# Two attention blocks and an expert layer on one core: intermediate results kept in PSUM, one wait moved, weight units rounded earlier

## What is computed

```python
z = rms_norm(x) @ w_in                     # q, c_kv, q_idx, k_idx, w_idx, g_attn, x_rnn, g_rnn, merge
s_idx = sum_j relu(q_idx[j] @ k_idx.T) * w_idx[j]          # 8 index heads, then the 64 best keys
o     = softmax(q_lat @ c_sel.T - slope * dist) @ c_sel    # 16 heads on the normalised latent c_kv
h     = rg_lru(conv4(x_rnn))               # u = b + sum of 4 taps; gates tanh(u @ w_rg)
x     = rms_norm(x + (g_a * (o * silu(g_attn)) @ w_proj + g_r * (h * silu(g_rnn)) @ w_rproj) @ w_out)
h2    = rmsnorm(x);  x = x + mixed(moba_attention(h2), mla_attention(h2))     # 8 + 8 heads
x     = rmsnorm(x + hierarchical_moe(rmsnorm(x)))          # 32 experts, 2 per token
```

## Time and profile before

| what | us |
|---|---|
| median of 3 runs | 736.76 (736.65 to 737.17) |
| profiled execution, its time | 739.29 |
| profiled execution, its span | 737.4 |
| PE busy | 662.7 (90%) |
| DVE busy | 397.5 (54%) |
| ACT busy | 327.3 (44%) |
| POOL busy | 394.2 (53%) |
| chain that ended last | PE 46%, DVE 25%, DMA 16%, ACT 5% |
| HBM read | 179.73 MB, 245 GB/s over the span |

### The profile page before, as it was taken

How to read it: one execution, slowest core, us unless ns; L and a number is a source line. 1 busy time by engine, 2 the same in 40 slices (tenths; PEclk the granted TensorE clock), 3 DMA queues, 4 the chain that set the end, 5 groups by cost and what they waited for, 6 DMA issues and landing times.

```text
span 737.4 us, 13811 instructions
## 1 busy us (share of the span) xinstructions
PE 662.7 (90%) x5600; PEld 553.8 (75%) x5600; DVE 397.5 (54%) x672; ACT 327.3 (44%) x599; POOL 394.2 (53%) x284
## 2 busy tenths in 40 slices
PE   3999989989999999989999999999999986786763
PEld 3999879889989999988779999999655443443321
DVE  6799954699995247997955655533322111111102
ACT  7556657855653456564358755451211110011003
POOL 3889657687879989798799665881000000000000
PEclk9999999999999999999999999998999998899997
DMA  8755333433444555434364434999799999999992
GB/s 346 276 171 173 115 114 124 160 119 122 165 122 165 179 196 196 171 127 161 115 216 132 154 128 148 374 424 384 287 424 419 423 418 424 420 421 422 421 417 85
DMA packets 26130, 181.72 MB, mean 246 GB/s; under 512 B 2896, under 2 KB 3152, under 8 KB 4688
## 3 DMA queue, kind: packets, MB, share of 16 engines
q1 hardware_dynamic: 25488, 179.22, 63.6%
q10 hardware_dynamic: 576, 1.57, 0.6%
HBM read 179.73 MB, written 1.05 MB: 245 GB/s over the span
## 4 chain that ended last, share of the span: by engine, by line
PE 46%; DVE 25%; DMA 16%; ACT 5%; issue 4%; POOL 2%; SPq 2%; ACTq 0%; DVEq 0%
PE D L446 25%; DMA big<-w_expert_dram 7%; DVE big L1440 6%; PE L L881 4%; DMA ring<-w_expert_dram 4%; DMA attn<-w_expert_dram 4%; POOL ring_r L1423 2%; DVE small L1440 2%; SPq L387 2%; PE L L861 2%; PE QB L914 2%; DVE hT L1440 2%; PE L L603 2%; DVE big_r L1459 1%; DVE big_r L1464 1%
## 5 line engine op out<-in xcount | busy, mean ns | idle before, releaser
L1423 POOL TENSOR_TENSOR ring_r<-ring,ring_r 128x512 fp32r<-128x512 f32 x280 | 394.0, 1442 | 105.3 <-ACT ring_r L1030 105.2
L446 PE MATMUL D<-scr_r,ring_r 128*128 128x256 f32 x1104 | 213.1, 289 | 0.8 <-DVE big L1440 0.8
L1030 ACT ACTIVATE ring_r<-ring 128x1024 fp32r<-128x1024 f32 x140 | 146.2, 1053 | 75.7 <-PE D L446 68.5
L446 PEld LDWEIGHTS D<-scr_r,ring_r 128*128 128x128 f32 x1104 | 175.4, 191 | 3.4 <-issue 2.1
L446 PE MATMUL D<-hT_r,ring_r 128*128 128x256 f32 x552 | 156.1, 283 | 0.0
L446 PE MATMUL D<-big_r,ring_r 128*128 128x256 f32 x1110 | 138.5, 285 | 1.6 <-POOL ring_r L1423 1.6
L446 PEld LDWEIGHTS D<-big_r,ring_r 128*128 128x128 f32 x1110 | 135.0, 192 | 3.7 <-issue 2.8
L446 PEld LDWEIGHTS D<-hT_r,ring_r 128*128 128x128 f32 x552 | 105.8, 192 | 1.2 <-issue 1.0
L1440 DVE SCALAR_TENSOR_TENSOR th<-th,L 64x256 f32<-64x256 f32 x32 | 13.4, 418 | 136.6 <-ACT th L1345 136.0
L1345 ACT ACTIVATE th<-L 64x256 f32<-64x256 f32 x16 | 6.0, 377 | 91.8 <-PE L L881 91.8
L881 PE MATMUL L<-big,small 128*32 128x256 f32 x432 | 33.3, 412 | 12.3 <-DMA big<-w_expert_dram 9.3
(11 more groups left out here) (358 smaller groups left out, 1011.7 us busy)
## 6 DMA issues: line engine op xcount, KB each, us to landing
ring<-w_dense_dram SPq DMA_DIRECT2D x69, 1024.0 KB, 4.9
big<-w_expert_dram SPq DMA_DIRECT2D x40, 1024.0 KB, 26.3
ring<-w_expert_dram SPq DMA_DIRECT2D x30, 1024.0 KB, 26.5
wu<-w_expert_dram SPq DMA_DIRECT2D x6, 1024.0 KB, 25.3
scr<-w_expert_dram SPq DMA_DIRECT2D x5, 1024.0 KB, 21.8
hT<-w_expert_dram SPq DMA_DIRECT2D x5, 1024.0 KB, 23.9
attn<-w_expert_dram SPq DMA_DIRECT2D x5, 1024.0 KB, 24.1
xT<-w_expert_dram SPq DMA_DIRECT2D x5, 1024.0 KB, 26.0
```

The source lines that it names most:

```text
L446: last = mm(out_, r32(w[i][ws]), r32(x[j][xs_]), start=start and m == 0, stop=stop and m == 2)
L1030: A_(r32(hi_unit(j)), dense_unit(j), ACT.Copy).then_inc(hi_ready, 1)
L1423: last = g.tensor_tensor(r32(w), w, r32(h).bitcast(F32), ALU.subtract)
```

## The change

1. PE's first chunk takes the rest of the weight before the rest of x.
2. The relu of the index scores is written in place in PSUM; DVE reads the scores there; PE waits for the accumulation (`idx_acc`) instead of the relu before it overwrites a bank.
3. The norm of the latent moves behind the index selection on DVE, and its wait on PE moves from ahead of the q units to `values(0)`.
4. The convolution's sums stay in PSUM banks QB, UB, L0, L1 until the last tap. `rg_gates` therefore waits for all eight sums. `rg_gates` 0 and 1 come after q unit 5, the others within q units 6 and 7, after their third and sixth block and at their end. ACT takes `rg_tanh` 0 to 6, then `q_in(3)`, then 7.
5. Logits stay in banks L0 and L1 through bias, maximum and exp; `normalise` reads them there and writes E; `score_pair` waits for the previous pair's `probs` instead of its `biased`.
6. Attention outputs are gated in PSUM and split from there; `head_out` goes.
7. At the entry of the second block ACT rounds one unit ahead of the first piece of the hidden state and one each ahead of the second and third.
8. `uq` units are rounded 768 columns wide, and one of each pair before the wait for its second unit.

```diff
...
+        CB = [QB, UB, L0, L1]
...
+        def width(n):
+            return QC * P if 0 <= n - UNIT0["uq"] < H2 else UNIT
...
-            def chunk(stage, c, src, kc=DC, split=None, per=2):
+            def chunk(stage, c, src, kc=DC, split=None, per=2, between=None):
+                if between:
+                    for k in range(kc):
+                        last = mm3(dst, w, src, np.s_[:, k * P:(k + 1) * P], np.s_[:, k, :], k == 0, k == kc - 1)
+                        if k in (2, 5):
+                            between(k // 3)
+                    last.then_inc(unit_done, 1)
+                    between(2)
+                    return
...
+                pe.wait_ge(lo_ready, 1)
+                for k in range(DC):
+                    mm(dst, r32(w[1][:, k * P:(k + 1) * P]), r32(x0_hi[:, k, :]), start=False, stop=False)
-                    mm(dst, r32(w[0][:, k * P:(k + 1) * P]), r32(x0_lo[:, k, :]), start=False, stop=False)
-                pe.wait_ge(lo_ready, 1)
-                for k in range(DC):
-                    last = mm(dst, r32(w[1][:, k * P:(k + 1) * P]), r32(x0_hi[:, k, :]), start=False, stop=(k == DC - 1))
+                    last = mm(dst, r32(w[0][:, k * P:(k + 1) * P]), r32(x0_lo[:, k, :]), start=False, stop=(k == DC - 1))
...
-                        pe.wait_ge(idx_relu, j - 2)
+                        pe.wait_ge(idx_acc, j - 2)
...
-                pe.wait_ge(conv_done, c + 1)
-                pe.wait_ge(idx_relu, IDXH)
+                pe.wait_ge(conv_done, 8)
...
-                pe.wait_ge(v1_ready, n - 1) if n >= 2 else pe.wait_ge(idx_relu, IDXH)
+                pe.wait_ge(v1_ready, n - 1) if n >= 2 else pe.wait_ge(idx_acc, IDXH)
+                if n == 0:
+                    pe.wait_ge(normed, NM0[N_CKV] + 1)
-            pe.wait_ge(normed, NM0[N_CKV] + 1)
-                chunk("q", c, h2)
+                chunk("q", c, h2, between=(lambda i: rg_gates(3 * c - 16 + i)) if c >= 6 else None)
-                if c >= 6:
-                    for i in range(4 * (c - 6), 4 * (c - 6) + 4):
-                        rg_gates(i)
+                if c == 5:
+                    rg_gates(0)
+                    rg_gates(1)
-                pe.wait_ge(biased, a) if a else pe.wait_ge(gates, 8)
+                pe.wait_ge(probs, a) if a else pe.wait_ge(gates, 8)
...
+            def o_bank_emptied(n):
+                for name, size in (("o", 8), ("ob", 4), ("oa", 4)):
+                    if n <= size:
+                        break
+                    n -= size
+                pe.wait_ge(lo_of[name], n)
-                    pe.wait_ge(o_ready, a // 2 - 1)
+                    o_bank_emptied(a // 2 - 1)
...
-            pe.wait_ge(o_ready, 8)
+            pe.wait_ge(lo_of["o"], 8)
...
-                    pe.wait_ge(o_ready, 16)
+                    pe.wait_ge(lo_of["oa"], 4)
...
-                    A_(r32(hi_unit(j)), dense_unit(j), ACT.Copy).then_inc(hi_ready, 1)
+                    w = np.s_[:, 0:width(j)]
+                    A_(r32(hi_unit(j)[w]), dense_unit(j)[w], ACT.Copy).then_inc(hi_ready, 1)
...
+                if i == 2:
+                    act.wait_ge(idx_acc, IDXH)
-                    last = A_(u[:, c, :], bank[:, m * T:(m + 1) * T], ACT.Identity, bias=V("conv_b", c),
-                              scale=V("conv_w", 3 * 8 + c))
+                    last = A_(CB[i][:, m * T:(m + 1) * T], bank[:, m * T:(m + 1) * T], ACT.Identity,
+                              bias=V("conv_b", c), scale=V("conv_w", 3 * 8 + c))
-                    if j >= 4:
-                        act.wait_ge(idx_acc, j - 3)
-                    A_(scores_in[:, j % 4, :], IB[j % 4][:, 0:CAUSAL], ACT.Relu).then_inc(idx_relu, 1)
+                    A_(IB[j % 4][:, 0:CAUSAL], IB[j % 4][:, 0:CAUSAL], ACT.Relu).then_inc(idx_relu, 1)
...
-            for c in range(4):
+            for c in range(7):
-            for c in range(4, 8):
-                rg_tanh(c)
+            rg_tanh(7)
...
-                if a >= 2:
-                    act.wait_ge(pt_mm, a - 1)
-                    last = A_(E[:, a % 2, c0:c0 + n], S[:, a % 2, c0:c0 + n], ACT.Exp,
+                    last = A_(LB[a % 2][:, c0:c0 + n], LB[a % 2][:, c0:c0 + n], ACT.Exp,
...
-            round_pieces("att2", hT, scr, lambda i: act.wait_ge(normed, NM0[N_FIN1] + 2 * i + 2))
+            advance(UNIT0["cq"] + 5 + HI_UNITS)
+            def hidden_ready(i):
+                if i:
+                    advance(UNIT0["cq"] + 5 + min(i, 2) + HI_UNITS)
+                act.wait_ge(normed, NM0[N_FIN1] + 2 * i + 2)
+            round_pieces("att2", hT, scr, hidden_ready)
...
+                advance(UNITS_AT[FILL0["uq"] + i] - 1 + HI_UNITS)
...
-                    cols = np.s_[:, half * UNIT // 2:(half + 1) * UNIT // 2]
+                    cols = np.s_[:, half * width(n) // 2:(half + 1) * width(n) // 2]
...
-            dve.wait_ge(rel["dve"], 1)
-            norm(N_CKV, lambda c: zc[:, 0, :], lambda c: cT, "kv_norm_gain")
...
-                    last = stt(acc, scores_in[:, j % 4, c0:c0 + n], widx[:, tt, j:j + 1],
+                    last = stt(acc, IB[j % 4][:, c0:c0 + n], widx[:, tt, j:j + 1],
...
+            dve.wait_ge(rel["dve"], 1)
+            norm(N_CKV, lambda c: zc[:, 0, :], lambda c: cT, "kv_norm_gain")
+                taps = CB[c // 2][:, (c % 2) * T:(c % 2 + 1) * T]
-                    ins = stt(u[:, c, :], xr[:, c, 1 + t:1 + t + T], V("conv_w", t * 8 + c), u[:, c, :],
+                    ins = stt(taps if t else u[:, c, :], xr[:, c, 1 + t:1 + t + T], V("conv_w", t * 8 + c), taps,
...
-                if a >= 2:
-                    dve.wait_ge(expd, a - 1)
-                sa = S[:, a % 2, :]
+                sa = LB[a % 2][:, 0:CAUSAL]
-                    ins = stt(sa, Dm, float(2.0 ** (-8.0 * (a + 1) / H1)), LB[a % 2][:, 0:CAUSAL], ALU.mult, ALU.add)
+                    ins = stt(sa, Dm, float(2.0 ** (-8.0 * (a + 1) / H1)), sa, ALU.mult, ALU.add)
-                    ins = stt(sa, LB[a % 2][:, 0:CAUSAL], MOBA_SCALE if a < H1 + H2 else MLA_SCALE,
+                    ins = stt(sa, sa, MOBA_SCALE if a < H1 + H2 else MLA_SCALE,
-                    last = v.reduce_max(stat[:, a % 2, 0, tt:tt + 1], S[:, a % 2, c0:c0 + n], axis=AX.X, negate=True)
+                    last = v.reduce_max(stat[:, a % 2, 0, tt:tt + 1], sa[:, c0:c0 + n], axis=AX.X, negate=True)
+                if a >= 2:
+                    dve.wait_ge(pt_mm, a - 1)
-                    last = v.tensor_scalar(E[:, a % 2, c0:c0 + n], E[:, a % 2, c0:c0 + n],
+                    last = v.tensor_scalar(E[:, a % 2, c0:c0 + n], LB[a % 2][:, c0:c0 + n],
...
-                stt(oT[:, n, :], o_bank(n)[:, 0:T], 0.5, sg[:, n, :]).then_inc(o_ready, 1)
+                step(stt(o_bank(n)[:, 0:T], o_bank(n)[:, 0:T], 0.5, sg[:, n, :]))
+            def split_bank(name, lo, hi, i, bank):
+                v.tensor_copy(r32(hi[:, i, :]), bank).then_inc(hi_of[name], 1)
+                dve.wait_ge(hi_of[name], i + 1)
+                v.tensor_tensor(r32(lo[:, i, :]), bank, r32(hi[:, i, :]).bitcast(F32), ALU.subtract).then_inc(lo_of[name], 1)
-                dve.wait_ge(o_ready, n + 1)
-                split("o", oT, o_hi, n)
+                split_bank("o", oT, o_hi, n, o_bank(n)[:, 0:T])
...
-            def head_out(n):
+            def head_split(n):
-                dst = oB if n < 4 else oA
-                v.tensor_copy(dst[:, n % 4, :], o_bank(n)[:, 0:T]).then_inc(o_ready, 1)
-            def head_split(n):
-                dve.wait_ge(o_ready, 8 + n + 1)
-                split(*(("ob", oB, ob_hi) if n < 4 else ("oa", oA, oa_hi)), n % 4)
+                split_bank(*(("ob", oB, ob_hi) if n < 4 else ("oa", oA, oa_hi)), n % 4, o_bank(n)[:, 0:T])
-                if m >= 2:
-                    head_out(m - 2)
...
-            head_out(7)
+            head_split(7)
-            head_split(7)
```

More of the change, by code:

```diff
@@ L174, in build @@
         wuv = at(wu, K, H1, HD1)
-        S = at(attn, 0, 2, CAUSAL)
         E = at(attn, 2 * CAUSAL, 2, CAUSAL)
@@ L204, in build @@
         sq1 = at(small, 2 * K + 512, 2, T)
-        scores_in = at(attn, 0, 4, CAUSAL)
         cqT = at(big, 0, QC, T)
@@ L288, in build @@
         logits, biased, maxed, expd, probs = [sem(n) for n in ("logits", "biased", "maxed", "expd", "probs")]
-        pt_mm, pt_ready, o_mm, o_ready = [sem(n) for n in ("probs_transposed", "pt_ready", "o_matmul", "o_ready")]
+        pt_mm, pt_ready, o_mm = [sem(n) for n in ("probs_transposed", "pt_ready", "o_matmul")]
         mixed = sem("mixed_ready")
```

## The result

The changed kernel takes **729.75 us** (median, 729.01 to 731.38), the kernel before 736.96 in the same comparison: a ratio of 0.9899, 95% interval 0.9883 to 0.9914, or 7.2 us less. The forecast was 731.6 within 726.1 to 735.3.

A forecast was written before the change was run, and what follows sets the result against it. PE bounds the dense part and the expert weights' DMA the later stretch, in series. Terms -1.0 - 0.4 - 3.9 + 1.65 - 2.1 + 0.55 = -5.2 us from 736.76 gave 731.6 us, range 726.1 to 735.3.

The forecast's parts named there:

- The price of a PSUM operand beside POOL: DVE instructions: 0.41 us for 256 columns with a PSUM operand, 1.4 us staying in SBUF while POOL works.
- First chunk: PE's first chunk: taking the weight's rest before x's rest starts unit 1 1.8 us earlier; gain taken as 1.0 us.
- Gates: Convolution gates: gain 0.4 us beyond the first chunk, as PE's first keys then wait for ACT's roundings and copy.
- First attention: First attention: DVE saves 3.3 us a pair, so waits of 2.8 and 0.8 us go; gain 3.9 us.
- Entry: Entry of the second block: POOL without its pause slows DVE's hidden state, PE starts later; loss 1.65 us.
- uq: uq units: three waits go as POOL's unit falls to 2.16 us and ACT starts sooner; gain 2.1 us.
- Second attention: Second attention: PE waits once for DVE's scaling before writing new logits; loss 0.55 us.
- slower rival: Convolution: writing PSUM keeps taps at 0.88 us, PE waits 9.2 us at gate 0; 740.6 us, chance 0.06.
- unslowed hidden state: Second block's entry: DVE's hidden state isn't slowed beside POOL, a gain of 3.1 us; 726.9 us, chance 0.20.
- worse entry: Second block's entry: rests slowed too, 733.5 us; with one attention wait staying, 735.3 us; chance 0.12.
- hidden stream: Experts: the end of the expert weights' stream doesn't follow PE, so nothing changes; 736.8 us, chance 0.06.
- PSUM writes at 0.88: Convolution: the slower rival's claim that taps writing PSUM still take 0.88 us each; chance 0.06.

The follow-up runs named there:

- conv_sbuf: Changed kernel with the convolution's sums back in SBUF, the order of the gates left as changed; 738.50 us, ratio 1.0020.
- gates_early: Changed kernel with one of ACT's two roundings ahead of the sixth tanh, the other behind the last copy of queries; 727.44 us, ratio 0.9866.
- attention_sbuf: Changed kernel with the first attention's logits, exp and scaling, and its gated outputs and their split, back in SBUF; 732.79 us, ratio 0.9932.
- undo_uq: Changed kernel with part 8 undone: uq units 1024 columns wide and none rounded before ACT's wait; 732.19 us, ratio 0.9939.
- undo_entry: Changed kernel with part 7 taken back, so the second block's entry rounds its weight units where the kernel before did; 727.49 us, ratio 0.9872.
- best: Changed kernel with gates_early's edit, part 7 undone, ACT's bank copy before the first piece, PE's products with rounded weights first; 726.54 us, ratio 0.9869.

## Why the prediction was right, point by point

- **The price of a PSUM operand beside POOL** decided the case, and held: 476 and 422 ns as against 873 and 1244, 0.48 us a tap (taken: 0.445 with the step). conv_sbuf measures the other end, 0.87. A tap came out 0.04 us dearer than taken since the row of 0.41 has a constant as its scalar; the trace before had the closer form too, a 128x256 instruction at 40.15 us with one PSUM operand and a scalar for each partition, at 484 ns. The Trainium skill, page "VectorE: DVE Perf Modes", section "The TRN2 errata", gives a PSUM source 62 fixed cycles more than an SBUF source, an estimated 0.065 us. For this form the traces don't agree: 0.475 us from SBUF without POOL, 0.48 with a PSUM operand.
- **First chunk**, 1.0 taken, 1.55 measured. A head start at half rate was said to be worth half, "if the rate rises when it does now". In this trace it rose 1.9 us earlier, as in the other end of the bound. But that instant varies by 3 us among the traces with this first chunk, so how near the term came is luck: 0.9 to 1.6 by the thirteen traces.
- **Gates**, 0.4 taken, 0.1 measured. The mechanism is the one forecast: ACT's two roundings took 2.00 us from 94.57 and its copy 0.60, and PE started at 97.16. gates_early shows that the stall was this one. No run takes back parts 1 to 3. That DVE's taps begin at 68.28 instead of 76.72 and end before PE asks for them is read from the trace, as was forecast (70.2 and 80.9).
- **First attention**, 3.9 and 3.9. attention_sbuf returns it. But the step that shared it out, 1.6 us of a round for the scalings and 1.7 for the outputs, does not mean that each is worth half of the gain: each alone would have brought three quarters of it. The scalings saved 1.35 by the groups' means (873 to 476 ns and 631 to 351, two of each).
- **Entry**, a loss of 1.65 taken, 2.9 measured. Its steps hold to 0.1 us: counted from the same instant as before, the last piece ends at 313.14 + 5.54 = 318.7 (taken 318.75) and PE starts at 319.2 (319.3). What failed is that the sum stops where PE starts: 15 matmuls at half rate cost 1.46 us more.
- **uq**, 2.1 taken, 2.6 measured, returned by undo_uq (2.5). The sentence on POOL's unit made it look like a matter of width; the runs show either edit alone to be nearly enough.
- **Second attention**, 0.55 and 0.5: the scaling ended where it was put.
- **The wait before the third rotation**, 1.35 us, stood in no term, and it went. The rows show how; first POOL, DVE and ACT of before, then DVE and ACT of undo_entry:

```profile
344.72 5.21 POOL L1423 TENSOR_TENSOR ring_r<-ring,ring_r 128x512 fp32r<-128x512 f32 x4 [1.97 <-ACT ring_r L1030]
...
348.31 1.91 DVE L1440 SCALAR_TENSOR_TENSOR big<-big,vec,rinv 128x256 f32<-128x256 f32 x2
...
343.06 0.63 ACT L1039 ACTIVATE big_r<-big 128x512 fp32r<-128x512 f32 x1 [1.60 <-DVE big L1440]
...
343.57 0.88 DVE L1458 SCALAR_TENSOR_TENSOR big<-big,vec,rinv 128x256 f32<-128x256 f32 x2
...
336.89 0.63 ACT L1059 ACTIVATE big_r<-big 128x512 fp32r<-128x512 f32 x1 [0.17 <-DVE big L1458]
```

  Before, DVE's six instructions on the latent query took 7.97 us beside a POOL at work (after: 4.54, in undo_entry 6.5). ACT waited 1.60 us for their last result and only then rounded the next weight units; so POOL's four halves began later and the last of them ran beside DVE's second scaling of the latent key, which took 1.51 us instead of 0.48. That is 1.0 us. In undo_entry POOL was through at 343.57, just as DVE's pair began. The other 0.5 is the wide `uq` units: two instructions of the rotation took 1.07 and 1.65 us beside them, 0.79 and 1.39 beside narrow ones, and undo_uq brought 0.5 back. The first part is read from rows and no run takes it by itself. **Open** is why the six met POOL otherwise: undo_entry has the entry of before and yet not this wait, but its clock fell behind the entry and that of before did not.

Three terms brought 2.7 us more than was taken (first chunk, rotation, uq), two 1.6 less (gates, entry). The total is closer than its terms, and that is in part luck: up to 480 us the terms were off by 1.3 us together but by 4.5 added up without their signs. In the slower rival two numbers don't fit: with a wait of 9.2 us the sum is some 4 us on the other side, not 3.6.

Of the rivals, the unslowed hidden state falls by 1.42 us an instruction, the worse entry did come in part (through the clock, not through the rests), the hidden stream falls by the first panel 6.3 us early, and PSUM writes at 0.88 by the taps.

## What to carry to other kernels

When DVE and POOL work at the same time, look at where each DVE operand lies before looking at its size: one source moved to PSUM halved the mean of an instruction here. First look whether POOL is at work there at all: without it the scaling is quicker from SBUF (0.35 us against 0.476). Ask of any edit that keeps an engine busier who was living in its pause; part 7 filled POOL's pause and cost 2 us. Two edits against one wait should be tried each alone and both together, since their worth does not add.

## What the runs showed of the hardware

- The granted clock behind a short stop of PE is not one number. After the same 2.5 us of standing still it was 1.00 in one trace and 0.64 in another; after 4.5 us between 12 and 26 matmuls ran at 0.215 us, in nine kernels whose entry was the same; once, in best, it fell behind 1.7 us too (0.58 over 4 us), and after 4.5 us in conv_sbuf PE first ran some steps at the full rate before it fell. Where it fell, 12 to 26 matmuls at 0.215 instead of 0.12 us cost 1.1 to 2.5 us beyond the stop's length. Whether this makes the spread between executions is not shown.
- DVE instructions with one SBUF source were slowed beside POOL as well (the scaling 1.40 us against 0.35 without POOL, the cast of 256 columns 1.17 against 0.29, both in the trace before), not only those with two; the Trainium skill, page "SBUF — State Buffer", section "Who interferes with whom", puts `tensor_scalar` and casts among those that can take the shared port pair, and the trace agrees.
